# A two-layer streaming encoder step: output-weight splits, memory outputs, broadcasts and stores moved to other places in the engines' programs

## The chip, the cores and the metric

One core of a Trainium2 chip runs the whole program. The metric is the device time of one execution in microseconds (us). Five engines run in parallel, each with its own instruction list: PE (matmuls), DVE (VectorE), ACT (ScalarE), POOL (GpSimd) and SP (which here only issues DMAs). They wait for one another on semaphores that are written out by hand.

## The reference, cut to what matters

```python
def macaron_half(x, g, w_in, w_out):
    a, b = jnp.split(rms_norm(x, g) @ w_in, 2, axis=-1)
    return x + 0.5 * ((jax.nn.silu(a) * b) @ w_out)

# layer 0: macaron half -> mix -> macaron half
#   mix: q, k, v, qm = split(rms_norm(x) @ w_in_a)        (3*768 + 256 columns), q, k, qm rms-normed by head
#        6 differential heads (two softmaxes, p0 - lam*p1) || 4 memory heads over 256 memory rows
#        x = x + concat(heads, memory) @ w_out[0]
# shared k, v and log-forget values from rms_norm(x) @ w_kv
# layer 1: macaron half -> mix -> macaron half
#   mix: 12 forgetting-attention heads over the shared k, v || 4 memory heads
#        x = x + concat(heads, memory) @ w_out[1]
# memory keys and values of both layers: rms_norm(mem) @ w_mkv[l], keys rms-normed by head
```

There are 256 prompt rows and 64 sample rows (320 together), d = 1024, d_ff = 2816, head size 64. All is float32. New keys, values, log-forget values and memory keys and values are outputs too.

## The kernel before, in words

Activations stand transposed (128 features by 320 rows per tile). Every float32 product is made of three matmuls of 128x128 by 128x320 with rounded parts: `whi*xhi`, `whi*xlo` and `wlo*xhi`. So each block of weights is loaded to `raw`, ACT rounds it to `whi` (`split_hi`, L981, or in halves `split_half`, L990), and DVE subtracts to get `wlo` (`split_lo`, L1327; `split_half`, L1337).

The stages follow one another in the order of the table `STAGES`: in0, mkv0, mkv1, out0, pa, wo0, in1, out1, kv, in2, out2, pb, wo1, in3, out3. "in" and "out" are the two projections of a macaron half, "pa" and "pb" the projections before the attentions, "wo0" and "wo1" the output weights behind them. Weights pass through two slots; `raw`, `whi` and `wlo` have one buffer for each slot. SP loads pair i of a stage (a block for slot 0, one for slot 1) once DVE has split pair i-1 (`load_pair`, L381: it waits for `lo_ready`). In an out stage one output tile uses one pair, and a tile is 66 matmuls.

SP's program is one list. Around out0 it loads pairs 0 to 6 of out0, then waits until the memory keys and values of layer 0 and then of layer 1 are final (`aux_free`; the DVE finishes layer 0's behind out0's tile 1 and layer 1's behind tile 3, L1368), stores them (four stores, L396), issues four cache loads (L418 to L421), and then loads pair 7. At the end it stores y in four parts of two tiles.

In pa (20 output tiles) PE broadcasts head norms by small matmuls (`head_broadcast`, L513) into two banks behind tiles 11, 12, 13 (keys, two each) and 16, 17 (queries 0 to 3). DVE uses what was broadcast (L1368 for keys, L1375 for queries) behind tiles 12, 13, 14 and 17, 18; a bank is free for the next broadcast only when DVE has used it.

Each attention has nine units. In layer 0 six head units come first and three memory units last; in layer 1 units 0 to 2 are the memory and 3 to 8 the heads. For unit i: PE makes scores; DVE takes their negated maxima (`maxima`, L1524); ACT makes exponentials and their sums (`exps`, L1142); DVE takes reciprocals (`invert`, L1536) and scales the first bank's weights (L1544), POOL the second bank's (`normalise`, L1895); PE transposes them (L684; in layer 0's heads it multiplies by a diagonal, L681); ACT copies the first half of the result and DVE the second (L1152, L1557); PE multiplies by the values (L702 to L709); DVE copies the output (`out_tile`, L1564 and L1575), ACT rounds it and POOL subtracts. DVE and ACT also carry the query norms and the halves of the output weights of slots 0 and 1 (`split_half`, in units 1 to 4 of layer 0 and 4 to 7 of layer 1). PE's transposes of unit i of layer 1 wait also for DVE's use of a query broadcast (`aux_by`), since the banks are shared.

Of the kernel before, what the change touches and what calls it, by code (L numbers as in the profile page):

```python
# [23 lines left out]
ACT = mybir.ActivationFunctionType  # L24
AX = mybir.AxisListType

P = 128
# [123 lines left out]
def encoder_kernel(nc, a):  # L151

    ctx = ExitStack()
    with ctx:
# [220 lines left out]
        def _(sp):  # L375
# [19 lines left out]
            def store(dst, src):  # L395
                sp.dma_start(dst, src).then_inc(d_out, 16)  # L396
                stores[0] += 1
# [13 lines left out]
            load_stage("out0", 0, 7)  # L411

            for layer in range(2):
                st = f"mkv{layer}"
                sp.wait_ge(aux_free, AUX0[st] + 4)
                store(a["o_mkT"][layer].rearrange("(k p) r -> p k r", p=P), kmT[:, layer])
                store(a["o_mv"][layer].rearrange("(k p) r -> p k r", p=P), vm[:, layer])
            sp.dma_start(ckT[:], a["cakT"].rearrange("(k p) r -> p k r", p=P)).then_inc(d_cache_a, 16)  # L418
            sp.dma_start(cv[:], a["cav"]).then_inc(d_cache_a, 16)
            sp.dma_start(cmk[:], a["cmkT"][0].rearrange("(k p) r -> p k r", p=P)).then_inc(d_cache_a, 16)  # L420
# [34 lines left out]
            for q in range(0, KD, 2):  # L455
                sp.wait_ge(acc_free, TILE0["out3"] + q + 2)
                store(y_v[:, q:q + 2], x[:, q:q + 2])
# [510 lines left out]
        def _(act):  # L968
# [161 lines left out]
            def attention(layer):  # L1130
# [46 lines left out]
                def run_heads_first():  # L1177
                    exps(1, 0)
                    for i in range(len(units)):
                        if i == 7:  # L1180
                            head_root("sub", R)
                            copy_first(i)
                        exps(i + 1, 1)
                        if i != 7:
                            copy_first(i)
                        if i >= 1:
                            out_hi(i - 1)
                        if i == 1:
                            head_root("pa_m", R)
                        exps(i + 2, 0)  # L1190
                        if 1 <= i < 5:
                            split_half("wo0", i - 1)
                    sub_tiles_hi(range(6))
                    out_hi(len(units) - 1)

                def run_memory_first():
                    copy_first(0)
                    exps(1, 0)
                    exps(1, 1)
                    head_root("pb_q", R)  # L1200
                    copy_first(1)
                    out_hi(0)
                    exps(2, 0)
                    exps(2, 1)
                    copy_first(2)
                    out_hi(1)
                    exps(3, 0)
                    exps(3, 1)
                    out_hi(2)
                    exps(4, 0)  # L1210
                    for i in range(3, len(units)):
                        exps(i + 1, 1)
                        copy_first(i)
                        if i >= 4:
                            out_hi(i - 1)
                        exps(i + 2, 0)
                        if 4 <= i < 8:
                            split_half("wo1", i - 4)
                    out_hi(len(units) - 1)

# [91 lines left out]
        def _(dve):  # L1312
# [189 lines left out]
            def attention(layer):  # L1502
# [26 lines left out]
                def invert(i, bank):  # L1529
# [7 lines left out]
                    if unit["kind"] == "diff" or bank == 1:  # L1537
                        last.then_inc(rc_ready, 1)
                        return
# [5 lines left out]
                    last.then_inc(w_first, 1)  # L1545
# [47 lines left out]
                def run_heads_first():  # L1593
# [9 lines left out]
                    for i in range(len(units)):  # L1603
# [17 lines left out]
                        if 1 <= i < 5:  # L1621
                            split_half("wo0", i - 1)
# [3 lines left out]
                def run_memory_first():  # L1626
# [7 lines left out]
                    invert(1, 1)  # L1634
                    out_tile(0)
# [5 lines left out]
                    invert(2, 1)  # L1641
                    dve.wait_ge(zeroed, 3)
                    queries(0)
                    out_tile(1)
                    copy_second(2)
                    queries(1)
                    maxima(3, 0)
                    maxima(3, 1)
                    queries(2)
                    invert(3, 0)  # L1650
                    invert(3, 1)
                    out_tile(2)
                    maxima(4, 0)
                    maxima(4, 1)
                    for i in range(3, len(units)):
                        copy_second(i)
                        invert(i + 1, 0)
                        maxima(i + 2, 0)
                        invert(i + 1, 1)
                        maxima(i + 2, 1)  # L1660
                        if i < 6:
                            queries(i)
                        out_tile(i)
                        if 4 <= i < 8:
                            split_half("wo1", i - 4)
# [80 lines left out]
            def after_pa(j):  # L1746
                if 12 <= j < 15:
                    head_scale("pa_k", AUX0["pa_k"] + 2 * j - 24, lambda k: qk[:, 6 + k, :], lambda k: hgain("ka"), R,
                               [2 * j - 24, 2 * j - 23])
                if 17 <= j < 19:  # L1750
                    dve.wait_ge(zeroed, 1)
                    for q in (2 * j - 34, 2 * j - 33):
                        query_tile(AUX0["pa_q"] + q, qk[:, q, :], q, "qa")
# [82 lines left out]
        def _(pool):  # L1836
# [35 lines left out]
            def attention(layer):  # L1872
                units, u0 = UNITS[layer], NU * layer

                def normalise(i):
# [15 lines left out]
                    pool.wait_ge(rc_ready, u + 7)  # L1891
# [224 lines left out]
```

## Time and profile before

| | us |
|---|---|
| median of 3 runs | 1326.36 (1325.6 to 1330.48) |
| the profiled execution | 1334.7 |
| its span, first to last instruction | 1332.9 |
| PE busy in it | 1291.3 (97%) |
| DVE busy | 756.2 (57%) |
| ACT busy | 552.3 (41%) |
| POOL busy | 171.1 (13%) |

The span is the part that the trace shows; the execution's own time is 1.8 us longer. PE is busy nearly all the time, so what can be read for a change are the places where it is not: its idle stretches, what ended each, and the stretches with a lower granted clock. The mean granted clock of the execution is 0.991.

### The profile page before, as it was taken

The page shows a single profiled execution, that of the slowest core. Times are in us where ns is not written, and L with a number is a line of the kernel's source. Part 1 is how long each engine was busy: PE and PEld are TensorE (multiplying, and loading weights), DVE is VectorE, ACT ScalarE, POOL GpSimd, SP SyncE. Part 2 cuts the span into 40 slices and gives each one's busy share as a digit, 9 for nine tenths or more (in the row PEclk, how much of TensorE's full clock was granted, in tenths as well). Part 3 has the DMA queues.
Part 4 walks back from the last instruction along what each step waited for, and adds up shares of the span by engine and source line. Part 5 has one row for each costly group of instructions (what it writes and reads, how often), then busy time and mean ns, then how long its engine had stood idle before and what let it go on. Part 6 is the DMA issues. An engine that isn't in the chain of part 4 may idle for free.

```text
span 1332.9 us, 22047 instructions
## 1 busy us (share of the span) xinstructions
PE 1291.3 (97%) x8593; PEld 1259.6 (95%) x8593; DVE 756.2 (57%) x1167; ACT 552.3 (41%) x797; POOL 171.1 (13%) x205
## 2 busy tenths in 40 slices
PE   7999999999999999999999999999998899999999
PEld 6999999999887999999999989999997699999998
DVE  6755665455576655554455565554456846555533
ACT  7443353343264534333344333333353544343322
POOL 0200020055014100000131000000043420000000
PEclk9999999999899999999999999999999899999999
DMA  7454354553103444454444334454440034344343
GB/s 262 162 168 145 142 170 135 202 186 130 63 33 105 148 155 157 142 176 140 134 176 170 122 112 137 153 158 155 154 169 17 32 126 145 142 155 157 111 150 126
DMA packets 39210, 187.41 MB, mean 141 GB/s; under 512 B 4304, under 2 KB 14288, under 8 KB 23920
## 3 DMA queue, kind: packets, MB, share of 16 engines
q1 hardware_dynamic: 37824, 183.38, 40.1%
q0 software_dynamic: 1184, 3.13, 1.0%
q8 instruction: 39, 0.64, 0.2%
q10 hardware_dynamic: 144, 0.11, 0.0%
q14 instruction: 19, 0.16, 0.0%
HBM read 179.70 MB, written 6.90 MB: 140 GB/s over the span
## 4 chain that ended last, share of the span: by engine, by line
PE 91%; DVE 4%; DMA 1%; ACT 1%; issue 1%; POOL 1%; SPq 1%; ACTq 0%; DVEq 0%
PE bank L472 27%; PE bank L473 27%; PE bank L474 26%; PE bank L824 1%; PE bank L825 1%; PE bank L826 1%; PE bank L651 1%; DVE wlo L1327 1%; PE bank L681 1%; ACT whi L981 1%; DMA raw<-in_w_ffn_in 1%; PE outs L706 1%; PE bank L513 1%; DMA raw<-in_w_ffn_out 1%; POOL ew L1895 1%
## 5 line engine op out<-in xcount | busy, mean ns | idle before, releaser
L472 PE MATMUL bank<-xhi,whi 128*128 128x320 f32 (+1 forms) x1760 | 550.0, 313 | 12.5 <-DVE wlo L1677 7.9
L474 PE MATMUL bank<-xhi,wlo 128*128 128x320 f32 (+1 forms) x1760 | 546.3, 310 | 0.0
L473 PE MATMUL bank<-xlo,whi 128*128 128x320 f32 (+1 forms) x1760 | 546.3, 310 | 0.0
L1327 DVE TENSOR_TENSOR wlo<-raw,whi 128x2048 fp32r<-128x2048 f32 (+1 forms) x179 | 368.7, 2060 | 241.5 <-ACT whi L981 241.5
L981 ACT ACTIVATE whi<-raw 128x2048 fp32r<-128x2048 f32 (+1 forms) x179 | 307.9, 1720 | 257.9 <-PE bank L474 250.6
L472 PEld LDWEIGHTS bank<-xhi,whi 128*128 128x128 f32 x1760 | 333.6, 190 | 16.9 <-issue 12.8
L473 PEld LDWEIGHTS bank<-xlo,whi 128*128 128x128 f32 x1760 | 333.6, 190 | 0.5
L474 PEld LDWEIGHTS bank<-xhi,wlo 128*128 128x128 f32 x1760 | 333.4, 189 | 0.0
L472 PE MATMUL bank<-hhi,whi 128*128 128x320 f32 x704 | 219.3, 312 | 2.9 <-DVE wlo L1327 2.7
L473 PE MATMUL bank<-hlo,whi 128*128 128x320 f32 x704 | 217.5, 309 | 0.0
L474 PE MATMUL bank<-hhi,wlo 128*128 128x320 f32 x704 | 217.5, 309 | 0.0
L472 PEld LDWEIGHTS bank<-hhi,whi 128*128 128x128 f32 x704 | 132.1, 188 | 6.0 <-DVE wlo L1327 5.2
L473 PEld LDWEIGHTS bank<-hlo,whi 128*128 128x128 f32 x704 | 132.2, 188 | 0.0
L474 PEld LDWEIGHTS bank<-hhi,wlo 128*128 128x128 f32 x704 | 132.1, 188 | 0.0
L1078 ACT ACTIVATE hhi<-hid 128x320 f32 (+1 forms) x88 | 40.7, 463 | 132.5 <-DVE hid L1445 132.5
L1070 ACT ACTIVATE silu<-gate 128x320 f32<-128x320 f32 x88 | 40.7, 463 | 112.6 <-DVE gate L1437 112.6
L1437 DVE TENSOR_TENSOR gate<-bank,r 128x320 f32<-128x320 f32 x88 | 42.5, 488 | 77.4 <-PE bank L474 76.9
L1848 POOL TENSOR_TENSOR ssum<-ssum,sq 128x320 f32<-128x320 f32 (+1 forms) x42 | 39.2, 933 | 239.2 <-ACT sq L1106 191.7
L1449 DVE TENSOR_TENSOR hlo<-hid,hhi 128x320 f32 (+1 forms) x88 | 43.8, 498 | 30.8 <-ACT hhi L1078 30.8
L1442 DVE TENSOR_TENSOR up<-bank,r 128x320 f32<-128x320 f32 x88 | 42.9, 488 | 25.6 <-PE bank L474 25.6
L1103 ACT ACTIVATE xhi<-x,early 128x320 fp32r<-128x320 f32 (+1 forms) x24 | 13.5, 563 | 98.1 <-DVE x L1471 98.1
L1471 DVE SCALAR_TENSOR_TENSOR x<-bank,x 128x320 f32 (+1 forms) x32 | 15.7, 491 | 60.5 <-PE bank L474 60.5
(206 smaller groups left out, 1104.7 us busy)
## 6 DMA issues: line engine op xcount, KB each, us to landing
raw<-in_w_ffn_in SPq DMA_DIRECT2D x87, 1024.0 KB, 4.7
raw<-in_w_ffn_out SPq DMA_DIRECT2D x64, 704.0 KB, 4.1
raw<-in_w_in_a SPq DMA_DIRECT2D x10, 1024.0 KB, 4.7
raw<-in_w_out SPq DMA_DIRECT2D x8, 1024.0 KB, 4.7
raw<-in_w_kv SPq DMA_DIRECT2D x6, 1024.0 KB, 4.7
raw<-in_w_mkv SPq DMA_DIRECT2D x4, 1024.0 KB, 4.8
raw<-in_w_in_b SPq DMA_DIRECT2D x4, 1024.0 KB, 4.7
x<-in_xT SPq DMA_DIRECT2D x4, 320.0 KB, 5.4
```

The source lines that it names most:

```text
L472: mm(acc, wh, mhi(ks[q]), start=start and q == 0, stop=False)
L473: mm(acc, wh, mlo(ks[q]), start=False, stop=False)
L474: last = mm(acc, wl, mhi(ks[q]), start=False, stop=stop and q == nk - 1)
L981: nc.scalar.activation(whi[slot][:, 0:size], raw[slot][:, 0:size], ACT.Copy).then_inc(hi_ready[slot], 1)
L1070: nc.scalar.activation(silu[:, c, :], gate[:, c, :], ACT.Silu).then_inc(silu_out, 1)
L1078: nc.scalar.activation(hhi[:, bass.ds(2 * i + c, 1), :], hid[:, c:c + 1, :], ACT.Copy).then_inc(hh_ready, 1)
L1327: tt(wlo[slot][:, 0:size], raw[slot][:, 0:size], f32(whi[slot][:, 0:size]), ALU.subtract).then_inc(lo_ready[slot], 1)
L1437: tt(gate[:, c, :], banks[c][:, 0:R], r[:], ALU.mult).then_inc(acc_free, 1)
L1442: tt(up[:, c, :], banks[2 + c][:, 0:R], r[:], ALU.mult).then_inc(acc_free, 1)
L1449: tt(hlo[:, bass.ds(2 * i + c, 1), :], hid[:, c:c + 1, :], f32(hhi[:, bass.ds(2 * i + c, 1), :]), ALU.subtract).then_inc(hl_ready, 1)
L1471: stt(out=xd, in0=banks[q][:, 0:R].unsqueeze(1), scalar=0.5, in1=xd, op0=ALU.mult, op1=ALU.add).then_inc(acc_free, 1)
L1848: nc.gpsimd.tensor_tensor(ssum[:, 0:w], ssum[:, 0:w], sq[:, k % 2, 0:w], ALU.add).then_inc(ssum_step, 1)
```

## The change

Five places change. SP: the two memory stores of each layer and the cache loads stand between the loads of out0's pairs 4, 5, 6 and 7; y's last two tiles are stored one by one. DVE in pa: what was broadcast is used behind the same tile (11 to 13, and 16 and 17). Layer 0: the halves of the output weights are split in units 3 to 6 in place of 1 to 4. Layer 1: ACT copies the outputs of units 0 to 2 (`out_copy`) in place of DVE; DVE scales both banks of units 1 and 2 (POOL leaves them out); the maxima of unit 3 come ahead of query 1; of the output weights only slot 0 is split in halves (ACT in units 5 and 6, DVE in units 7 and 8, there ahead of the output copy), slot 1 as a whole behind the last unit.

```diff
@@ SP
-            load_stage("out0", 0, 7)
+            load_stage("out0", 0, 4)
             for layer in range(2):
                 st = f"mkv{layer}"
                 sp.wait_ge(aux_free, AUX0[st] + 4)
                 store(a["o_mkT"][layer].rearrange("(k p) r -> p k r", p=P), kmT[:, layer])
                 store(a["o_mv"][layer].rearrange("(k p) r -> p k r", p=P), vm[:, layer])
+                load_stage("out0", 4 + layer, 5 + layer)
             ...
+            load_stage("out0", 6, 7)
             ...
             load_stage("out0", 7)
             ...
-            for q in range(0, KD, 2):
-                sp.wait_ge(acc_free, TILE0["out3"] + q + 2)
-                store(y_v[:, q:q + 2], x[:, q:q + 2])
+            for q, end in ((0, 2), (2, 4), (4, 6), (6, 7), (7, 8)):
+                sp.wait_ge(acc_free, TILE0["out3"] + end)
+                store(y_v[:, q:end], x[:, q:end])
@@ ACT, layer 0
-                        if 1 <= i < 5:
-                            split_half("wo0", i - 1)
+                        if 3 <= i < 7:
+                            split_half("wo0", i - 3)
@@ ACT, layer 1
+                def out_copy(i):
+                    unit, u = units[i], u0 + i
+                    act.wait_ge(av_done, u + 1)
+                    for h in range(2):
+                        ...
+                        last = nc.scalar.activation(dst, o[:, :, h], ACT.Copy)
+                    last.then_inc(o_taken, 1)
                 def run_memory_first():
                     copy_first(0)
                     exps(1, 0)
                     exps(1, 1)
+                    out_copy(0)
                     head_root("pb_q", R)
                     ...
                     exps(2, 1)
+                    out_copy(1)
                     copy_first(2)
                     ...
                     exps(3, 1)
+                    out_copy(2)
                     out_hi(2)
                     ...
-                        if 4 <= i < 8:
-                            split_half("wo1", i - 4)
+                        if 5 <= i < 7:
+                            split_half("wo1", i - 5)
                     out_hi(len(units) - 1)
+                    split_hi(1, PAIR0["wo1"], BLK, acc_ready, TILE0["wo1"])
@@ DVE, invert
-                    if unit["kind"] == "diff" or bank == 1:
+                    if (unit["kind"] == "diff" or bank == 1) and not scaled:
                         last.then_inc(rc_ready, 1)
                         return
                     ...
-                    last.then_inc(w_first, 1)
+                    last.then_inc(w_second if scaled else w_first, 1)
@@ DVE, layer 0
-                        if 1 <= i < 5:
-                            split_half("wo0", i - 1)
+                        if 3 <= i < 7:
+                            split_half("wo0", i - 3)
@@ DVE, layer 1
                     invert(1, 0)
-                    invert(1, 1)
-                    out_tile(0)
+                    invert(1, 1, True)
                     ...
-                    invert(2, 1)
+                    invert(2, 1, True)
                     dve.wait_ge(zeroed, 3)
                     queries(0)
-                    out_tile(1)
                     copy_second(2)
-                    queries(1)
                     maxima(3, 0)
                     maxima(3, 1)
-                    queries(2)
+                    queries(1)
                     invert(3, 0)
                     invert(3, 1)
-                    out_tile(2)
+                    queries(2)
                     ...
+                        if i >= 7:
+                            split_half("wo1", i - 7)
                         out_tile(i)
-                        if 4 <= i < 8:
-                            split_half("wo1", i - 4)
+                    split_lo(1, PAIR0["wo1"], BLK)
@@ DVE, after_pa
-                if 12 <= j < 15:
-                    head_scale("pa_k", AUX0["pa_k"] + 2 * j - 24, ...)
-                if 17 <= j < 19:
-                    for q in (2 * j - 34, 2 * j - 33):
+                if 11 <= j < 14:
+                    head_scale("pa_k", AUX0["pa_k"] + 2 * j - 22, ...)
+                if 16 <= j < 18:
+                    for q in (2 * j - 32, 2 * j - 31):
@@ POOL, normalise
-                    pool.wait_ge(rc_ready, u + 7)
+                    if layer and i in (1, 2):
+                        return
+                    pool.wait_ge(rc_ready, u + 7 if u <= NU else u + 5)
```

## Rows read from the trace of the kernel before

**Rows 1.** The page's first part: busy time, share of span, instructions.

```profile
PE 1291.3 (97%) x8593; PEld 1259.6 (95%) x8593; DVE 756.2 (57%) x1167; ACT 552.3 (41%) x797; POOL 171.1 (13%) x205
```

**Rows 2.** Stretches: length; busy PE, PEld, DVE, ACT, POOL (instructions); PEclk; DMA share; GB/s.

```profile
349.00:357.00 8.00, 5.64 (x20) 5.08 (x20) 2.58 (x5) 0.00 (x0) 0.00 (x0) 0.64 0.12 52
...
366.00:420.00 54.00, 48.92 (x310) 40.68 (x309) 40.59 (x144) 32.41 (x105) 18.08 (x32) 1.00 0.24 76
1010.00:1030.00 20.00, 16.53 (x77) 12.34 (x77) 13.71 (x51) 8.59 (x30) 5.77 (x10) 0.91 0.01 1
1030.00:1040.00 10.00, 8.35 (x41) 6.93 (x41) 7.72 (x37) 6.63 (x28) 5.26 (x12) 0.83 0.00 0
1040.00:1056.00 16.00, 14.98 (x92) 12.40 (x90) 15.41 (x57) 9.19 (x30) 5.14 (x7) 1.00 0.08 19
1056.00:1069.00 13.00, 8.26 (x40) 6.26 (x39) 7.55 (x18) 5.61 (x16) 5.72 (x7) 0.87 0.30 109
```

**Rows 3.** Timeline of all engines in out0: start, length; in brackets idle before.

```profile
238.74 0.87 DVE L1368 SCALAR_TENSOR_TENSOR kmT<-kmT,early,bank 128x256 f32<-128x256 f32 x2
...
244.69 0.49 DVE L1471 SCALAR_TENSOR_TENSOR x<-bank,x 128x320 f32<-128x320 f32 x1 [1.67 <-PE bank L474]
...
249.84 0.40 SPq L396 DMA_DIRECT2D o_mkT<-kmT  x1
...
255.63 3.55 SPq L381 DMA_DIRECT2D raw<-in_w_ffn_out  x2
...
263.67 1.38 ACT L981 ACTIVATE whi<-raw 128x1408 fp32r<-128x1408 f32 x1 [6.52 <-DMA raw<-in_w_ffn_out]
265.08 1.63 DVE L1327 TENSOR_TENSOR wlo<-raw,whi 128x1408 fp32r<-128x1408 f32 x1 [6.27 <-ACT whi L981]
...
266.76 0.41 PE L472 MATMUL bank<-hhi,whi 128*128 128x320 f32 x1 [2.74 <-DVE wlo L1327]
```

**Rows 4.** The page's DMA issues: out<-in, count, size of one, us to landing.

```profile
raw<-in_w_ffn_out SPq DMA_DIRECT2D x64, 704.0 KB, 4.1
```

**Rows 5.** Timeline of PE and DVE in pa.

```profile
327.73 0.78 PE L513 MATMUL bank<-rs,select 64*128 64x320 f32 x2 [0.83 <-DVE qk L1368]
...
349.54 2.24 DVE L1375 SCALAR_TENSOR_TENSOR qz<-qk,early,bank 64x320 f32<-64x320 f32 x4
350.78 0.38 PE L513 MATMUL bank<-rs,select 64*128 64x320 f32 x1 [1.69 <-DVE qz L1375]
351.83 0.63 PE L513 MATMUL bank<-rs,select 64*128 64x320 f32 x1 [0.67 <-DVE qz L1375]
```

**Rows 6.** Timeline of layer 0's attention.

```profile
382.61 1.23 DVE L1337 TENSOR_TENSOR wlo<-raw,whi 128x1024 fp32r<-128x1024 f32 x1
384.27 0.53 PE L513 MATMUL bank<-rs,select 64*128 64x320 f32 x2 [0.91 <-issue]
...
396.57 1.04 ACT L990 ACTIVATE whi<-raw 128x1024 fp32r<-128x1024 f32 x1
...
408.53 1.10 PE L702 MATMUL outs<-pt,vm 128*128 128x512 f32 x2 [0.83 <-ACT pt L1152]
```

**Rows 7.** Timeline of layer 1's attention.

```profile
1019.90 0.62 DVE L1544 TENSOR_SCALAR ew<-ew,rc 128x256 f32<-128x256 f32 x2
1020.69 1.83 POOL L1895 TENSOR_SCALAR ew<-ew,rc 128x256 f32<-128x256 f32 x2 [4.59 <-DVE rc L1536]
1021.63 0.86 DVE L1575 COPY qk<-outs 64x256 f32<-64x256 f32 x2
...
1033.47 0.76 PE L684 MATMUL bank<-early,ew 128*128 128x128 f32 x4 [1.19 <-POOL ew L1895]
...
1060.42 1.29 PE L706 MATMUL outs<-pt,vrow 128*128 128x512 f32 x2 [2.17 <-DVE pt L1557]
...
1066.69 1.10 PE L706 MATMUL outs<-pt,vrow 128*128 128x512 f32 x2 [1.75 <-DVE pt L1557]
```

**Rows 8.** Timeline of SP: the last store of y.

```profile
1330.23 0.37 SPq L396 DMA_DIRECT2D o_yT<-x  x1
```

More of the change, by code:

```diff
@@ L1190, in run_heads_first @@
                         exps(i + 2, 0)
-                        if 1 <= i < 5:
-                            split_half("wo0", i - 1)
+                        if 3 <= i < 7:
+                            split_half("wo0", i - 3)
                     sub_tiles_hi(range(6))
                     out_hi(len(units) - 1)
+                def out_copy(i):
+                    unit, u = units[i], u0 + i
+                    act.wait_ge(av_done, u + 1)
+                    for h in range(2):
+                        half = slice(HD * h, HD * h + HD)
+                        if unit["kind"] == "mem_s":
+                            o = OB[half, 0:256].rearrange("p (c e r) -> p c e r", c=2, e=2)
+                            dst = qk[half, 12:14, ROWS_P:R]
+                        else:
+                            o = OB[half, 0:4 * P].rearrange("p (c e r) -> p c e r", c=4, e=2)
+                            dst = out_tile_of(unit["tile"])[half, 0:256].rearrange("p (c r) -> p c r", c=4)
+                        last = nc.scalar.activation(dst, o[:, :, h], ACT.Copy)
+                    last.then_inc(o_taken, 1)
                 def run_memory_first():
@@ L1527, in maxima, with invert @@
                     last.then_inc(s_taken, 1)
-                def invert(i, bank):
+                def invert(i, bank, scaled=False):
                     if i >= len(units):
@@ L1746, in after_pa @@
             def after_pa(j):
-                if 12 <= j < 15:
-                    head_scale("pa_k", AUX0["pa_k"] + 2 * j - 24, lambda k: qk[:, 6 + k, :], lambda k: hgain("ka"), R,
-                               [2 * j - 24, 2 * j - 23])
-                if 17 <= j < 19:
+                if 11 <= j < 14:
+                    head_scale("pa_k", AUX0["pa_k"] + 2 * j - 22, lambda k: qk[:, 6 + k, :], lambda k: hgain("ka"), R,
+                               [2 * j - 22, 2 * j - 21])
+                if 16 <= j < 18:
                     dve.wait_ge(zeroed, 1)
-                    for q in (2 * j - 34, 2 * j - 33):
+                    for q in (2 * j - 32, 2 * j - 31):
                         query_tile(AUX0["pa_q"] + q, qk[:, q, :], q, "qa")
```

## The prediction

> **What bounds the kernel now.** I read the page's busy times first: PE is busy 1291.3 us of the span of 1332.9 [rows 1], so all that this change can win lies in the 42 us in which PE is idle and in the stretches at a lower clock. A busy PE is not PE at its peak, and here that is the clock: the stretches [rows 2] show where the granted clock is under 1.00, the higher of its two levels (2.4 GHz), because part of the stretch ran at the lower (1.2 GHz). From 349 to 357 us it is 0.64: 0.36 x 8 = 2.9 us of full-speed time are missing. In layer 1's attention 1010 to 1030 lacks 1.8 us, 1030 to 1040 1.7 and 1056 to 1069 1.7. Third, the waits in the timeline tell what each gap waited for [rows 3, 5 to 7]. The clock fell inside gaps of PE: the stretches of [rows 2] with a low clock are those that hold gaps of 1.2 to 2.2 us [rows 5, 7]. It did not fall at the gap of 2.74 us in out0 [rows 3], so a gap alone does not decide it.
>
> **Stores between the weight loads (out0).** What it removes: the loads of pair 7 start only at 255.63, behind four stores and four cache loads, and ACT gets the block at 263.67, so 8.0 us after its issue, where the median is 4.1 [rows 3, 4]. PE stands 2.74 us for it. With those transfers issued earlier this goes: -2.74. What it adds: SP must now wait for layer 1's memory keys before it may issue pair 5. DVE ends these at 238.74 + 0.87 = 239.6 [rows 3], behind tile 3. Before, pair 5's loads went out when DVE had split pair 4, whose slot 0 was done some 7 us earlier (SP's list runs on, nothing was in its way). Now: 239.6, two stores of 0.40 and the steps between them 0.9, issue at 240.5; landing 4.1; ACT 1.38; DVE 1.63 [rows 3, 4]: 247.6 at the earliest. PE ends tile 4 at 244.7, where DVE takes it [rows 3], and needs the block then: it stands 2.9 us at least. The two stores (512 KB) are ahead of the load in the same queue. For pair 7, 2304 KB ahead cost 8.0 - 4.1 = 3.9 us, so 512 KB cost some 0.9, at most the whole 3.9. I take 0.9, nearest to it by size: a stall of 3.8 (2.9 to 6.8). Slot 1 of pair 5 is needed half a tile (about 4.8 us) later and is split in that time; layer 0's stores cost nothing, since DVE ends those keys while pair 3 and 4 wait for buffers anyway. A gap that long may drop the clock: the one of 1.69 in pa did, the one of 2.74 here did not. A low stretch like those in attention lacks 1.7 us, part of it inside the gap; I add 1.2. Sum: +3.8 - 2.7 + 1.2 = +2.3 (-0.5 to +5.8).
>
> The Trainium skill bears on the store term (DMA: Bandwidth & Descriptors, section on queues, rings and completion order): on each DMA engine the descriptors of a queue are consumed in ring order, whichever DMA they belong to. By that rule a weight load is behind every byte of the stores issued before it, and stores between loads are never free when the load has no slack. The 8.0 us of pair 7 agree.
>
> **Broadcasts used at once (pa).** PE stands 0.83 us at tile 12 [rows 5], and as long at 13 by the same pattern, because DVE frees a bank only behind the next tile; at tile 17 it stands 1.69 + 0.67 while DVE runs the 2.24 us of query products; at 19 some 0.5. Used behind the same tile, all have a whole tile of PE's time (24 matmuls, about 3.5 us) as cover: DVE needs 2.24 + 0.49 for it. All of 4.5 us goes. The clock then has no gap in which to fall: of the 2.9 us missing in 349 to 357, 0.5 lie in the gap itself, so 2.4 come back. Where DVE's time would be late instead: the maxima of the first unit behind tile 18, which now start earlier. -6.9 (-4.0, if the clock falls at another place, to -7.4).
>
> **Halves of the output weights in units 3 to 6 (layer 0).** Removed: DVE's half of 1.23 ahead of the copy that PE waits 0.91 for in unit 2 [rows 6], and by the same 1.2 us the queries that unit 3's transposes wait for: -1.2. Added: the same half in units 5 and 6, ahead of memory units, where POOL's scaling and ACT's copy are already late (PE stands 0.83 at 408.53 [rows 6]). There ACT makes its half (1.04) right behind the exponentials, DVE waits for it and then needs 1.23; DVE's next copy is about 1.2 later in unit 6, and ACT's second half ahead of the sub-norm's root and the copy adds 0.6 in unit 7: +1.8 (0 to 2 x 2.27 = 4.5). The gap before the values grows to over 1.5 us, near those with a lower clock: +0.4. Sum +1.0 (-1.2 to +3.5).
>
> **Layer 1's attention.** (a) Units 1 and 2: POOL's 1.83 become DVE's 0.62 [rows 7], and DVE gives 0.86 of copying to ACT, which is idle there. But DVE's extra 0.62 is ahead of query 0, for which the transposes of unit 2 wait. Net -0.3. (b) Unit 3: the maxima no longer stand behind query 1, which waits for a broadcast that PE makes only after all scores of unit 3. Exponentials, reciprocals and POOL's scaling come some 2 us earlier; PE's gap of 1.19 [rows 7] and one of 0.5 ahead of it go, and the transposes start right behind the scores of unit 4: -2.0. Without the gap the clock has less reason to fall: of 1.7 us in 1030 to 1040 I count 1.2. (c) Units 4 and 5: DVE is busy 15.41 of 16 us in 1040 to 1056 [rows 2], so a half of 1.23 [rows 6] out of its chain is worth up to that twice; PE itself is busy 14.98 of the 16, so only its 1.0 us of idle comes back: -0.9. (d) Units 6 to 8: PE is busy 8.26 of 13 us in 1056 to 1069 [rows 2]; it stands 0.8, 2.17 and 1.75 for copies behind splits [rows 7]. The chain transposes, copies, values stays, so about 2.0 of these 4.7 us stay: -2.7. Clock: -0.9 of 1.7. Slot 1's whole block costs ACT 1.9 and DVE 2.3 behind the last unit, but is needed only at tile 2 of the output projection, 48 matmuls or 7 us in; it is done about 1 us before. If that cover fails, it costs 1 to 3 us. Sum: -0.3 - 2.0 - 1.2 - 0.9 - 2.7 - 0.9 = -8.0; I take -7.3, since ACT's copies from the matmul banks have no row of their own (bounds: as DVE's 0.86, or nothing). Range -3 to -9.5.
>
> **End.** The last store is issued at 1330.23 [rows 8] and the span ends 2.7 us later; half of its 320 KB saves about 0.4.
>
> **Sum.** +2.3 - 6.9 + 1.0 - 7.3 - 0.4 = -11.3. The profiled execution took 1334.7, so its like would take 1323.4. The median of the runs is 8.3 lower than the profiled one; taken off 1326.4 it gives 1315.1. Some 5.5 us of the gain are clock, and a run that is faster than the profiled one may have fewer such stretches: I give 1 us back. **1316 us.**
>
> **Rivals.** Less gain: the clock falls as often as before, only elsewhere, and units 6 to 8 are bound by the chain of engines and not by the splits. Then 5.5 of clock and 1 of (d) are missing: 1322. For it: the clock did fall in gaps under 2 us, and many of those stay. Against: in layer 0's attention the clock stayed at 1.00 [rows 2] with gaps under 1 us.
>
> More gain: pair 5 is hardly late, since its block lands at 244.6 and the other terms hold, and (d) is whole: -11.3 - 3.0 - 2.0, 1310. Against it speaks the plain addition in out0.
>
> Slower: the stall in out0 does not stop at one load. With one buffer per slot every late load makes the next late. If each of the six loads of pairs 5 to 7 lands 8.0 us after issue as that of pair 7 did, and not 4.1, 6 x 3.9 = 23.4 replace the 3.8: +19.6, and the change is 8 us slower: 1334. It decides from an average landing of about 6.4 us (3.8 + 11.3 = 15.1 us over six loads, 2.5 each). For it: all caches and stores now fall between these loads. Against: the loads have some slack in a tile of 9.7 us, and there is less than a third of the traffic ahead of any of them.
>
> **How the numbers follow.** Forecast (1311 to 1319.7) 0.55; less gain 0.22; more gain 0.17; slower 0.06. A run of this kernel can tell 0.5% (6.6 us) from no change: faster means under 1319.7. Forecast, more gain and a small part of less gain: 0.75; same 0.19; slower 0.06. The range takes the forecast, most of both neighbours and the bounds of the out0 stall: 1308 to 1326.
>
> **What would show it.** Right: a gap of PE of 3 to 5 us ahead of out0's tile 5 and none ahead of tile 7; no gap at tiles 12, 13, 17 of pa and clock 1.00 there; no wait for POOL in unit 3 of layer 1; layer 1's attention about 7 us shorter; layer 0's attention as long as before or 1 us longer, with a larger gap ahead of the values of unit 7. Wrong: no gap at tile 5, a low clock in pa in spite of full work, or DVE still late in units 6 to 8.

## The result

Five executions of the changed kernel took 1319.43 us (median; 1318.83 to 1319.64), five of the kernel before beside them 1327.17 (1325.6 to 1330.48). The ratio is 0.9925 with an interval of 0.9904 to 0.9945: 7 to 13 us less. Forecast were 1316 and a gain of 10.3 us against the median. The profiled execution took 1318.83 us and its span is 1317.0, against 1334.7 and 1332.9 before.

The page's first part after (answers to [rows 1]). The span is 15.9 us shorter: PE is busy 6.3 us less with the same matmuls, and idle 9.6 us less (32.0 for 41.6).

```profile
PE 1285.0 (98%) x8593; PEld 1254.7 (95%) x8593; DVE 755.1 (57%) x1164; ACT 554.3 (42%) x802; POOL 168.7 (13%) x201
```

To see where, both traces are cut at the same instructions: out0 (first keys of layer 0's memory to the last x), pa (to layer 0's first product with a diagonal), layer 0's attention (to the first output projection), layer 1's attention. Columns as in [rows 2]. Length less busy PE is PE's idle time; more busy time for the same matmuls is mostly time at the lower clock (not all: see pa below). Before:

```profile
180.49:276.74 96.25, 92.79 (x646) 91.72 (x647) 49.15 (x65) 35.35 (x43) 13.78 (x17) 1.00 0.53 174
276.74:369.53 92.79, 87.67 (x559) 83.64 (x558) 51.26 (x84) 31.54 (x45) 39.62 (x41) 0.96 0.33 114
369.53:415.88 46.35, 42.39 (x275) 35.88 (x274) 35.86 (x131) 30.70 (x101) 11.86 (x19) 1.00 0.27 89
1009.36:1068.41 59.05, 48.18 (x244) 37.90 (x242) 44.49 (x161) 30.23 (x101) 22.05 (x35) 0.91 0.08 25
```

After:

```profile
179.93:279.93 100.00, 95.31 (x646) 94.24 (x647) 49.15 (x65) 35.36 (x43) 13.77 (x17) 0.97 0.52 168
279.93:364.15 84.22, 83.60 (x559) 80.75 (x558) 51.63 (x84) 31.54 (x45) 39.52 (x41) 1.00 0.36 125
364.15:411.60 47.45, 43.98 (x275) 36.38 (x275) 35.96 (x131) 30.63 (x101) 11.83 (x19) 0.96 0.22 71
1003.63:1053.02 49.39, 42.58 (x245) 33.61 (x242) 40.81 (x157) 30.47 (x105) 19.92 (x31) 1.00 0.00 1
```

The idle forecast of layer 1's attention is the -7.3 that was taken less the clock's -2.1; its parts had added up to -5.9.

| us | idle: forecast | idle: measured | slow clock: forecast | busy PE: measured | sum: forecast | sum: measured |
|---|---|---|---|---|---|---|
| out0 | +1.1 | +1.23 | +1.2 | +2.52 | +2.3 | +3.75 |
| pa | -4.5 | -4.50 | -2.4 | -4.07 | -6.9 | -8.57 |
| layer 0's attention | +0.6 | -0.49 | +0.4 | +1.59 | +1.0 | +1.10 |
| layer 1's attention | -5.2 | -4.06 | -2.1 | -5.60 | -7.3 | -9.66 |

The four stretches make -13.4 of the -15.9 us. The rest is 0.6 us less ahead of out0, 0.5 less behind layer 1's attention (the end of the span), and 1.45 of busy PE between the two attentions, where the change does nothing: that piece takes 593.48 us before and 592.03 after, but 593.47 in sp_fix, which has the change's edits too, so it is a difference between executions.

Out0's timeline, SP, ACT, DVE and PE (answers to [rows 3]). Pair 5 goes out at 240.01 behind the stores, and ACT has its block 4.9 us later. PE stands 3.98 us ahead of tile 5; its other waits in out0, at the start, are 0.76 and 0.19. Before (first row), the block for slot 0 of pair 5 was issued at 232.86; from out0's start that is 52.4 us, and now 60.1, so the issue moved by 7.7 us. With the 0.8 us more to landing that makes 8.5, of which some 4.5 were slack.

```profile
232.86 0.33 SPq L381 DMA_DIRECT2D raw<-in_w_ffn_out  x1
...
239.06 0.40 SPq L396 DMA_DIRECT2D o_mkT<-kmT  x1
239.49 0.47 SPq L396 DMA_DIRECT2D o_mv<-vm  x1
240.01 0.98 SPq L381 DMA_DIRECT2D raw<-in_w_ffn_out  x2
...
244.89 1.38 ACT L984 ACTIVATE whi<-raw 128x1408 fp32r<-128x1408 f32 x1 [8.31 <-DMA raw<-in_w_ffn_out]
...
246.37 1.63 DVE L1349 TENSOR_TENSOR wlo<-raw,whi 128x1408 fp32r<-128x1408 f32 x1 [7.34 <-ACT whi L984]
...
248.05 0.64 PE L475 MATMUL bank<-hhi,whi 128*128 128x320 f32 x1 [3.98 <-DVE wlo L1349]
```

Pa's timeline (answers to [rows 5]). The broadcasts have no bracket: PE came to them without idling. DVE uses a pair right behind.

```profile
330.03 0.56 PE L516 MATMUL bank<-rs,select 64*128 64x320 f32 x2
...
349.97 0.56 PE L516 MATMUL bank<-rs,select 64*128 64x320 f32 x2
350.49 1.11 DVE L1397 SCALAR_TENSOR_TENSOR qz<-qk,early,bank 64x320 f32<-64x320 f32 x2
```

PE's longest waits in layer 0's attention (answer to [rows 6]), both in unit 7, and in layer 1's (answer to [rows 7]). In layer 1's unit 3 PE no longer waits for POOL, and at the end of the attention it waits 1.20, 0.69 and 0.98 us.

```profile
401.75 0.66 PE L687 MATMUL bank<-early,ew 128*128 128x128 f32 x4 [1.25 <-POOL ew L1919]
403.86 2.04 PE L705 MATMUL outs<-pt,vm 128*128 128x512 f32 x2 [1.45 <-ACT pt L1155]
...
1011.18 1.10 PE L705 MATMUL outs<-pt,vm 128*128 128x512 f32 x2 [1.02 <-ACT pt L1155]
...
1016.03 1.07 PE L687 MATMUL bank<-early,ew 128*128 128x128 f32 x8 [2.23 <-DVE qz L1397]
...
1046.55 1.10 PE L709 MATMUL outs<-pt,vrow 128*128 128x512 f32 x2 [1.20 <-ACT pt L1155]
1049.65 0.66 PE L687 MATMUL bank<-early,ew 128*128 128x128 f32 x4 [0.69 <-POOL ew L1919]
1051.29 1.10 PE L709 MATMUL outs<-pt,vrow 128*128 128x512 f32 x2 [0.98 <-DVE pt L1580]
```

The waits of PE in layer 1's attention before that [rows 7] leaves out, in units 1 and 2, unit 3, and the later units:

```profile
1016.16 0.66 PE L684 MATMUL bank<-early,ew 128*128 128x128 f32 x4 [0.71 <-POOL ew L1895]
1017.65 1.10 PE L702 MATMUL outs<-pt,vm 128*128 128x512 f32 x2 [0.83 <-ACT pt L1152]
1021.70 0.63 PE L684 MATMUL bank<-early,ew 128*128 128x128 f32 x4 [1.56 <-DVE qz L1375]
...
1031.62 0.66 PE L684 MATMUL bank<-early,ew 128*128 128x128 f32 x4 [0.46 <-DVE ew L1544]
...
1051.47 1.07 PE L684 MATMUL bank<-early,ew 128*128 128x128 f32 x8 [0.92 <-issue]
...
1057.59 0.66 PE L684 MATMUL bank<-early,ew 128*128 128x128 f32 x4 [0.81 <-POOL ew L1895]
```

The last store (answers to [rows 8]) is issued 2.2 us before the span's end, where it was 2.7.

```profile
1314.82 0.34 SPq L396 DMA_DIRECT2D o_yT<-x  x1
```

### The profile page after: what moved, and what is told of

The parts are those of the page before. It is cut to its first block, busy times and chain, and to the rows that moved or that the text cites. A ratio compares the mean times of both kernels' runs of the same rounds, so it can differ in the third digit from the quotient of the medians.

```text
span 1317.0 us, 22024 instructions
## 1 busy us (share of the span) xinstructions
PE 1285.0 (98%) x8593; PEld 1254.7 (95%) x8593; DVE 755.1 (57%) x1164; ACT 554.3 (42%) x802; POOL 168.7 (13%) x201
## 4 chain that ended last, share of the span: by engine, by line
PE 93%; DVE 3%; ACT 1%; DMA 1%; issue 1%; POOL 1%; SPq 0%; ACTq 0%; DVEq 0%
PE bank L475 28%; PE bank L476 27%; PE bank L477 27%; PE bank L827 1%; PE bank L829 1%; PE bank L828 1%; PE bank L654 1%; PE bank L684 1%; DVE wlo L1349 1%; ACT whi L984 1%; PE outs L709 1%; PE bank L687 1%; PE bank L516 0%; DMA raw<-in_w_ffn_in 0%; ACT ew L1145 0%
```

## Experiments: one part alone, in the kernel before

The first four ran side by side, with 24 runs of the kernel before at a median of 1329.57 us (1325.01 to 1332.38).

**sp_only.** The order of loads and stores in out0 alone.

```diff
-            load_stage("out0", 0, 7)
+            load_stage("out0", 0, 4)
             for layer in range(2):
                 ...
+                load_stage("out0", 4 + layer, 5 + layer)
             ...
+            load_stage("out0", 6, 7)
```

> The kernel before with one part of the change: out0's pairs 4, 5 and 6 are loaded between the stores and the cache loads. Theory A (the wait for layer 1's memory keys starves pair 5): PE stands about 4 us ahead of out0's tile 5, the 2.7 us ahead of tile 7 go, the granted clock falls once for it, and the kernel is 2.5 to 4.5 us slower than before (ratio 1.002 to 1.0035). Rival B (the interleaving spreads the transfers and wins the 2.7 us): no gap at tile 5, 2 to 3 us faster (ratio 0.998).

1332.47 us, ratio 1.0034 (1.0015 to 1.0052): slower, as the theory has it. The gap at tile 5 (first row) is there with all else as before, and out0 takes 98.76 us for 96.25. The second row is layer 1's attention, which this kernel leaves alone: it took 55.47 us here and 59.05 in the trace before, of which 3.4 us are busy PE and only 0.2 idle PE.

```profile
246.67 0.41 PE L475 MATMUL bank<-hhi,whi 128*128 128x320 f32 x1 [3.71 <-DVE wlo L1330]
...
1007.40:1062.87 55.47, 44.82 (x244) 34.95 (x242) 44.27 (x161) 30.11 (x101) 22.00 (x35) 0.97 0.08 27
```

**pa_only.** The broadcasts used behind the same tile, alone (keys at tiles 11 to 13, queries at 16 and 17, as in the change's diff).

```diff
-                if 12 <= j < 15:
+                if 11 <= j < 14:
...
-                if 17 <= j < 19:
-                    for q in (2 * j - 34, 2 * j - 33):
+                if 16 <= j < 18:
+                    for q in (2 * j - 32, 2 * j - 31):
```

> The kernel before with one part of the change: in the projection ahead of layer 0's attention DVE uses each broadcast behind the same tile. Theory A (four bank waits and the low clock that starts in one of them): stretch of pa 7 to 8.5 us shorter in the trace, granted clock 1.00 there; timed 5 to 8 us faster (ratio 0.994 to 0.996). Rival B (waits alone, the clock falls elsewhere or was not low in the timed runs): 4 to 4.8 us (ratio 0.9965).

1323.06 us, ratio 0.9962 (0.9943 to 0.998), so 5 us. Pa takes 84.23 us, as in the changed kernel, at a clock of 1.00. The trace's 8.6 us hold the removal of a low stretch whose length varies: in sp_only, which leaves pa alone, the clock from 349 to 357 us was 0.79 for 0.64 and pa took 91.56 us for 92.79; in l1_only, which leaves it alone too, the clock there was 0.65.

```profile
275.39:359.62 84.23, 83.61 (x559) 80.76 (x558) 51.62 (x84) 31.54 (x45) 39.52 (x41) 1.00 0.35 125
```

**l1_only.** All of layer 1's edits alone (ACT's output copies, DVE's scaling, the order of the queries, the splits), as in the change's diff.

> The kernel before with one part of the change: everything in layer 1's attention (ScalarE copies units 0 to 2, DVE scales units 1 and 2, maxima of unit 3 first, splits in later units). Theory A: the attention is 7 to 10 us shorter, timed 6 to 10 us faster (ratio 0.9925 to 0.9955). Rival B (what the two traces show there is mostly clock, which the timed runs do not lose): 3 to 5 us (ratio 0.9965).

1323.29 us, ratio 0.9951 (0.9927 to 0.9975), so 6.5 us. Its attention takes 50.31 us, of which PE is idle 6.8, as in the changed kernel.

```profile
1009.58:1059.89 50.31, 43.51 (x245) 34.26 (x242) 40.79 (x157) 30.45 (x105) 19.92 (x31) 0.98 0.02 3
```

By ratios the three parts make +4.5 - 5.0 - 6.5 = -7 us, the whole -10 (-7 to -13). Each part has an interval of 2.5 to 3 us either way, and the edits in layer 0 and at the end are in none of them: no interaction can be made out.

## Experiments: the changed kernel without one part

**sp_fix.** Pair 5 goes out with pair 4, ahead of layer 1's stores.

```diff
-                load_stage("out0", 4 + layer, 5 + layer)
+                if layer == 0:
+                    load_stage("out0", 4, 6)
```

> The changed kernel with out0's pair 5 loaded ahead of layer 1's stores instead of behind them. Theory A (the one load that waits for the memory keys costs the whole gap at tile 5 and its clock): no gap at tile 5 nor at 7, out0 about 6.5 us shorter than in the changed kernel, ratio to the kernel before 0.9875 to 0.989. Rival B (the stores' bytes delay loads wherever they stand): a gap of 1 to 3 us moves to tile 6 or 7, and the ratio stays at 0.991 to 0.9925.

1312.63 us, ratio 0.9885 (0.9861 to 0.9909): some 5 us better than the change by the ratios, whose intervals overlap by 0.0005, and 6.5 by the traces' spans. Out0 (first row) has no gap left at tile 5 or 7, and 0.72 us idle in all; pa (second) is as in the change. Layer 0's attention (third) ran at full clock here and has 4.56 us of idle; layer 1's (last) is the same as the change's.

```profile
179.08:272.32 93.24, 92.52 (x646) 91.72 (x647) 49.24 (x64) 35.36 (x43) 13.78 (x17) 1.00 0.56 180
272.32:356.56 84.24, 83.62 (x560) 80.77 (x558) 51.63 (x84) 31.53 (x45) 39.56 (x41) 1.00 0.36 125
356.56:403.64 47.08, 42.52 (x276) 35.80 (x275) 35.93 (x131) 30.63 (x101) 11.86 (x19) 1.00 0.21 67
997.11:1046.50 49.39, 42.58 (x245) 33.59 (x242) 40.79 (x157) 30.46 (x105) 19.96 (x31) 1.00 0.00 1
```

So theory A holds. Its timeline says why: ACT takes pair 5's block as soon as PE frees the buffer, at the time of the stores, and DVE has split it at 241.6, 6 us before the changed kernel. The order ahead of the stores removes both the wait for the keys and the stores' bytes; that the wait is the larger part is worked out, not tested by itself: the wait had moved the issue by 7.7 us, and the landing took 0.8 more (4.9 for a median of 4.1).

```profile
238.22 0.40 SPq L396 DMA_DIRECT2D o_mkT<-kmT  x1
...
238.50 1.38 ACT L985 ACTIVATE whi<-raw 128x1408 fp32r<-128x1408 f32 x1 [2.75 <-PE bank L478]
...
239.99 1.63 DVE L1350 TENSOR_TENSOR wlo<-raw,whi 128x1408 fp32r<-128x1408 f32 x1 [1.79 <-ACT whi L985]
```

The next four take back one more part each from sp_fix, beside 11 runs of the kernel before at 1326.07 us. Sp_fix itself ran beside other runs (1329.57), so with it only ratios and traces are compared; among the four, times too.

**l0_back.** Layer 0's halves in units 1 to 4 again, on ACT and DVE alike.

```diff
-                        if 3 <= i < 7:
-                            split_half("wo0", i - 3)
+                        if 1 <= i < 5:
+                            split_half("wo0", i - 1)
```

> The kernel of sp_fix with layer 0's halves split in units 1 to 4 again, as before the change. Theory A (units 5 and 6 are no lighter: the halves there delay POOL's scaling and the copy for unit 7): layer 0's attention takes 46.3 us again in place of 47.1, so 0.8 us less, the wait ahead of unit 2's broadcast returns (0.9) and that ahead of unit 7's values shrinks to 0.8. Rival B (the trace's difference between the two was chance): attention as long as in sp_fix. Ratio to the kernel before 0.987 to 0.989; the timed runs cannot tell 0.8 us.

1312.99 us, ratio 0.9904 (0.9884 to 0.9925): by times nothing. In the trace the attention is 0.8 us shorter (46.28 for 47.08): the wait of 0.91 ahead of unit 2's broadcast is back, those in unit 7 have shrunk from 1.26 and 1.44 to 0.33 and 0.83.

```profile
371.55 0.52 PE L517 MATMUL bank<-rs,select 64*128 64x320 f32 x2 [0.91 <-issue]
...
394.32 0.66 PE L688 MATMUL bank<-early,ew 128*128 128x128 f32 x4 [0.33 <-POOL ew L1920]
395.81 1.10 PE L706 MATMUL outs<-pt,vm 128*128 128x512 f32 x2 [0.83 <-ACT pt L1156]
```

**split_back.** Layer 1's four halves in units 4 to 7 again, on ACT (shown) and on DVE, there behind the output copy.

```diff
-                        if 5 <= i < 7:
-                            split_half("wo1", i - 5)
+                        if 4 <= i < 8:
+                            split_half("wo1", i - 4)
                     out_hi(len(units) - 1)
-                    split_hi(1, PAIR0["wo1"], BLK, acc_ready, TILE0["wo1"])
```

> The kernel of sp_fix with layer 1's output weights split in four halves in units 4 to 7 again, everything else of layer 1 as changed. Theory A (the halves on DVE and ScalarE make the copies of units 5 to 8 late): attention of layer 1 3 to 4.5 us longer than the 49.4 of sp_fix, with waits of PE for the copies of units 7 and 8. Rival B (units 6 to 8 are bound by the chain of engines): at most 1.5 us longer.

1319.7 us, ratio 0.9948 (0.9931 to 0.9965): the largest step, 6 us more by ratio than l0_back beside it. The trace shows 10.25 us of idle PE in this attention for 6.81, and 3.1 us more busy time. Waits of 2.18 and 2.38 us for DVE's half of the copy come back, and from the first of them on the clock is low (0.73, then 0.66). Theory A's wait and place are right; the attention is 6.6 us longer, not 3 to 4.5, because of that clock.

```profile
1032.86 1.06 PE L688 MATMUL bank<-early,ew 128*128 128x128 f32 x8 [0.93 <-issue]
1038.97 0.66 PE L688 MATMUL bank<-early,ew 128*128 128x128 f32 x4 [0.81 <-POOL ew L1918]
1041.81 2.04 PE L710 MATMUL outs<-pt,vrow 128*128 128x512 f32 x2 [2.18 <-DVE pt L1580]
1048.65 2.04 PE L710 MATMUL outs<-pt,vrow 128*128 128x512 f32 x2 [2.38 <-DVE pt L1580]
```

**order_back.** Query 1 ahead of the maxima of unit 3 again, and query 2 ahead of its reciprocals.

```diff
+                    queries(1)
                     maxima(3, 0)
                     maxima(3, 1)
-                    queries(1)
+                    queries(2)
                     invert(3, 0)
                     invert(3, 1)
-                    queries(2)
```

> The kernel of sp_fix with query 1 ahead of the maxima of unit 3 and query 2 ahead of its reciprocals again. Theory A (the maxima waited behind a query that waits for a broadcast): PE waits again ahead of unit 3's transposes, attention of layer 1 1.5 to 2.5 us longer than 49.4, with a low clock 1 us more. Rival B (ScalarE's copies and the scaling on DVE bring the gain there): under 0.7 us longer.

1314.04 us, ratio 0.9913 (0.9892 to 0.9934), not to be told from sp_fix by times. The trace is clear: layer 1's attention takes 51.12 us for 49.39. Two waits of together 1.68 us are back, one of 0.34 is gone, and PE is idle 1.34 us more at a clock of 1.00.

```profile
1017.49 0.66 PE L688 MATMUL bank<-early,ew 128*128 128x128 f32 x4 [0.49 <-DVE ew L1568]
1019.34 0.66 PE L688 MATMUL bank<-early,ew 128*128 128x128 f32 x4 [1.19 <-POOL ew L1920]
```

**pool_back.** POOL scales units 1 and 2 again, and DVE copies the outputs of units 0 to 2.

```diff
-                    out_copy(0)
...
-                    invert(1, 1, True)
+                    invert(1, 1)
+                    out_tile(0)
...
-                    if layer and i in (1, 2):
-                        return
```

> The kernel of sp_fix with POOL scaling the second banks of units 1 and 2 and DVE copying the outputs of units 0 to 2 again; order and splits as changed. Theory A (worth little): attention of layer 1 0.3 to 1.2 us longer than 49.4. Rival B (the two are the heart of the gain in units 1 to 3): 2 us or more longer.

1315.39 us, ratio 0.9909 (0.989 to 0.9928): not to be told from sp_fix. PE is idle 7.51 us for 6.81. Its 52.10 us for 49.39 are otherwise a low stretch in this execution, at the last values of the attention, where this kernel has the same wait of 0.98 as sp_fix. The 0.7 us are one wait ahead of a query broadcast in unit 3 (second row), 1.08 for 0.34; the waits in units 1 and 2 add up to 3.3 us here and to 3.5 in sp_fix.

```profile
998.23:1050.33 52.10, 44.59 (x244) 34.47 (x242) 41.67 (x159) 28.34 (x99) 23.53 (x35) 0.97 0.02 6
...
1022.37 0.41 PE L517 MATMUL bank<-rs,select 64*128 64x320 f32 x1 [1.08 <-ACT pt L1156]
```

## Experiments: further steps from sp_fix

Beside 7 runs of the kernel before at 1330.96 us.

**l0_tail.** Layer 0 as layer 1: only slot 0 in halves (units 3 and 4), slot 1 as a whole at the end. ACT's side is shown; DVE does the same, with `split_lo` in unit 8.

```diff
-                        if 3 <= i < 7:
+                        if 3 <= i < 5:
                             split_half("wo0", i - 3)
...
+                    split_hi(1, PAIR0["wo0"], BLK, acc_ready, TILE0["wo0"])
```

> The kernel of sp_fix with layer 0's output weights done as the change does layer 1's: slot 0 in halves in units 3 and 4, slot 1 as a whole behind the last unit. Theory A (only the halves in units 5 and 6 cost): no wait ahead of unit 2's broadcast, those of units 7 and 8 at most 0.8 us, layer 0's attention 45.0 to 45.5 us in place of 47.1, and no wait of PE at tile 2 of the output projection. Rival B (slot 1 is ready too late): the attention is shorter by as much, but PE stands 1 to 3 us at tile 2. Ratio to the kernel before 0.986 to 0.9885 (A).

1312.47 us, ratio 0.9869 (0.9852 to 0.9887). Layer 0's attention takes 45.28 us, with all_three's 45.27 the least here, and PE is idle 2.99 of them: the 0.91 ahead of unit 2's broadcast is gone, and the 1.26 and 1.44 of unit 7 are 0.32 and 0.83. The whole block is split in time: PE doesn't wait in the output projection.

```profile
358.47:403.75 45.28, 42.29 (x276) 35.88 (x275) 33.69 (x129) 28.90 (x99) 11.85 (x19) 1.00 0.07 24
```

**q0_first.** Query 0 ahead of the scaling of unit 2's second bank.

```diff
-                    invert(2, 1, True)
                     dve.wait_ge(zeroed, 3)
                     queries(0)
+                    invert(2, 1, True)
```

> The kernel of sp_fix with query 0 ahead of the scaling of unit 2's second bank. Theory A (the transposes of unit 2 wait for query 0, and the 0.8 us of scaling that the change put ahead of it are in the way): PE's wait there falls from 2.2 to about 1.4 us, attention of layer 1 0.3 to 0.9 us shorter than 49.4. Rival B (the second bank's scaling is late then): the wait only splits in two, attention as long as before.

1312.54 us, ratio 0.9863 (0.9845 to 0.9881). The wait of 2.23 us is 1.50, so DVE's scaling was 0.7 of it, and PE is idle 6.10 us for 6.81, as theory A has it. The attention is not shorter for it in this execution but 2 us longer (51.39), since the clock fell twice: behind the 1.50, where the transposes took 1.93 us for 1.07, and at the last values.

```profile
999.02:1050.41 51.39, 45.29 (x244) 35.78 (x242) 40.91 (x157) 30.46 (x105) 19.97 (x31) 0.95 0.02 3
...
1010.70 1.93 PE L688 MATMUL bank<-early,ew 128*128 128x128 f32 x8 [1.50 <-DVE qz L1398]
```

**act_early.** ACT's halves in units 4 and 5, one unit earlier.

```diff
-                        if 5 <= i < 7:
-                            split_half("wo1", i - 5)
+                        if 4 <= i < 6:
+                            split_half("wo1", i - 4)
```

> The kernel of sp_fix with ScalarE's two halves of layer 1's output weights one unit earlier (4 and 5 instead of 5 and 6). Theory A (ScalarE's half in unit 6 stands ahead of the exponentials and the copy of unit 7): the wait of 1.2 us ahead of unit 7's values falls under 0.5, attention of layer 1 0.7 to 1 us shorter than 49.4. Rival B (PE waits there for the chain as such): under 0.3 us shorter.

1314.95 us, ratio 0.9887 (0.9869 to 0.9905). ACT's 1.20 became DVE's 0.98, POOL's 0.69 became 0.91, and the attention takes the same 49.39 us. The forecast of 0.7 to 1 us less was wrong and rival B right: these two of ACT's splits are not what PE waits for at the end. That what is left is the chain of copies and scaling is the likely reading; no run takes away the halves that DVE has in units 7 and 8.

```profile
1039.26 1.10 PE L710 MATMUL outs<-pt,vrow 128*128 128x512 f32 x2 [0.98 <-DVE pt L1581]
1042.58 0.66 PE L688 MATMUL bank<-early,ew 128*128 128x128 f32 x4 [0.91 <-POOL ew L1920]
```

**all_three.** The last three edits together.

> The kernel of sp_fix with the three edits together (layer 0's slot 1 whole at the end, query 0 first, ScalarE's halves one unit earlier). Theory A (they touch different waits and add up): layer 0's attention 45.3 us, layer 1's 47.5 to 48.3 us, median about 1309 to 1311, ratio to the kernel before 0.984 to 0.988. Rival B (they overlap or the clock falls more often): no faster than sp_fix, 0.9885 to 0.99.

1313.24 us (1310.2 to 1315.67), ratio 0.9864 (0.9843 to 0.9884). Layer 0's attention took 45.27 us, but layer 1's had two low stretches in the profiled execution (51.34 us, for a forecast of 47.5 to 48.3), and the median missed the forecast of 1309 to 1311. Sp_fix, l0_tail, q0_first and all_three can't be told apart by times; each is faster than both kernels of this case.

## Why the prediction came out as it did

**The direction and the size of the timed gain were right, the size in part by luck.** The -10.3 us forecast against the median lie in the interval (-7 to -13), and 1319.43 in the forecast's own range; its upper half, since the median moved by 7.7 only. The luck: in the traces the gain was underrated by 4.6 us, and in the step from the trace to the median 7 us too little were given back.

**Out0: the mechanism right, one term too small.** The loads of pair 5 waited for the memory keys, and behind 512 KB of stores one took 4.9 us to landing, where 4.1 + 0.9 were worked out. The stall was 3.98 for 3.8. The clock term is what was mis-sized: 1.2 us were added and 2.52 came. Sp_fix shows what the place costs in all: 93.24 us for 100.00. The cascade of late loads didn't come: after pair 5, ACT waited for PE to free the buffer and not for a load, so the slower rival was wrong at the step from one late load to the next. (Its threshold of 6.4 us doesn't follow from its sum either: 4.1 + 2.5 is 6.6.)

**Pa: the idle term exact, the clock term too small.** -4.5 us of idle were forecast and measured. Busy time fell by 4.07 us for 2.4. Some 0.9 of that is the broadcasts themselves (two pairs took 0.78 us each [rows 5] and take 0.56 now, the pair that was split 1.01 and now 0.56), and the low stretch ran on behind 357 us, where [rows 2] stop: from 357 to 362 the clock was 0.90, 0.5 us more.

**Layer 0: right by a partly wrong path.** At full clock (sp_fix, 4.56 us of idle, against 3.96 before) the halves' new places cost +0.6 us of idle, as forecast, and the remaining 0.4 was put down to the clock. In the changed kernel's execution a low stretch began at the second of unit 7's waits (granted clock 0.59 from 403.86 to 408 us) and brought +1.59 of busy time, and idle time went: the waits of 0.71 and 0.46 us that sp_fix has in unit 8 are not there, while the others are the same. L0_back confirms the sign: the move of these four halves is a small loss in the trace, 0.8 us.

**Layer 1: the parts.** PE's waits before and after can be set side by side. (a) -0.3 was forecast: those in units 1 and 2 are 3.3 us before (0.71, 0.83, 1.56 and 0.24) and 3.5 after (1.02, 0.26 and 2.23). ACT's copy, which had no row, took 0.77 us for DVE's 0.86. (b) -2.0 was forecast, but the two waits that it removes are 0.46 and 1.19 us, and one of 0.33 came: -1.3, and order_back has 1.3 more idle PE. Here the forecast took off more than the rows held. (c) -0.9 was forecast, and the wait of 0.92 is gone. (d) -2.7 was forecast: 4.7 us before, 2.9 after, so -1.9. Together -3.9 of the measured -4.06; so the idle terms of (a), (b) and (d) were too large by 2.0 us in all, of which 0.7 had been taken off beforehand.

Taken back one by one from sp_fix, the parts have 0.7, 1.3 and 3.4 us of idle PE, 5.5 together and not 4.06. The low clock of the trace before isn't the reason, since sp_only ran the same unchanged attention at 0.97 in place of 0.91 and PE was idle 10.65 us for 10.87. Split_back's last wait is 2.38 where the kernel before had 1.75 and sp_only 1.55: the four halves cost more beside the other edits than in the kernel before. Why is not shown.

The clock terms, -2.1, are the larger miss: the changed kernel has none of the low stretches, and busy PE fell by 5.60. The 1.8 us that 1010 to 1030 lacks were read from [rows 2] and then counted in no term. But 3.4 of the 5.60 are no gain of the change either: sp_only, with this attention as before, already has that much less busy PE, and pa_only, where it is as before too, has 1.1 more. The whole block at the end was covered, as worked out.

**The clock, taken over all.** Forecast was -2.9 us of clock and -8.4 of idle in the profiled execution; measured were -6.3 of busy PE and -9.6 of idle. The terms that were mis-sized are those of the clock. (The "5.5 us of clock" of the recorded sum are 4.5 by its own terms, 2.4 + 1.2 + 0.9; the 1 us given back rests on no row.) That is offset in the timed runs by the conversion to the median, where 1 us was given back: the gain of 15.9 us in the traces is 7.7 in the medians, so 8 us had to be given back. The profiled execution before, 1334.7 us at a mean clock of 0.991, was slower than each of the 47 timed runs of its kernel on record; those with 0.997 take 1324.6 to 1326.1 us. The five runs after all have 0.995, perhaps in part because of the new gap in out0. At the same 0.995 other runs of the kernel before took 1328.6 to 1330.2 us, so the change is worth about 10 us there. Of the rival "less gain", the clock did fall elsewhere, in out0 and layer 0, but it stayed at 1.00 in pa and layer 1's attention.

## What to carry to other kernels

Split a forecast of an engine-bound kernel into idle time and time at a lower clock: the first can be worked out from the waits (here to 0.1 us in out0 and pa, to about 1 us in the attentions), the second varies from run to run and must be judged over several executions, not against one profile; a piece of the kernel that the edit leaves alone, read in both traces, tells how much varies by itself. A store put between two loads delays the second by the wait for its data, not only by its bytes; if the load has no slack, put the store behind one more load. Work that no engine needs soon was cheaper behind the last unit of a chain that alternates between engines than in it (split_back, l0_tail).

## What had not been expected of the hardware

In these traces the clock is low behind some of PE's gaps and not behind others, and not by their length alone. Behind the gaps of 3.98 us (after) and 3.71 (sp_only) it was low; the gap of 2.74 in out0 [rows 3] left it at 1.00, that of 2.96 at the same tile in l1_only did not (0.72 over the next 6 us), and it was low behind 1.69 [rows 5] and 1.50 (q0_first). It was low at the last values of the attention in pool_back, behind a wait of 0.98, and not behind the same wait in sp_fix. Sp_fix with the same wait of 2.23 as the change ran layer 1's attention at 1.00, l0_back with that wait at 0.97 and 1.4 us longer. So one kernel without any change of its own spreads over 1325.0 us at a mean clock of 0.997 to 1332.4 at 0.991, and what decides in a single execution stays open.
